# Gate and up of two feed-forwards by seven block products instead of eight

## The reference, cut to what matters

```
h = rms_norm(x, norm_g)                               # 1024 x 1024
ff = silu(h @ w_gate) * (h @ w_up)                    # 1024 x 2816
x = x + scale * (ff @ w_down)                         # scale 1.0 (ffn0) or 0.5 (ffn2)
```

## Time and profile before

| | |
|---|---|
| median of 3 runs | 3575.89 us |
| profiled execution | 3575.58 us |
| its span, first to last instruction | 3573.8 us |
| TensorE matmul busy | 3481.6 us, 97% |
| vector engine busy | 1467.3 us, 41% |
| GpSimd busy | 1134.1 us, 32% |
| scalar engine busy | 963.1 us, 27% |
| granted TensorE clock, mean | 0.989 |
| moved by DMA | 218.31 MB |

### The profile page before, as it was taken

One profiled execution on the slowest core, in us unless ns is written; L12 is line 12 of the kernel. 1 busy time (PEld: TensorE's weight loads), 2 busy tenths in 40 slices (PEclk: granted clock), 3 DMA queues, 4 the chain that ended last, 5 costly groups with the idle time before them and its releaser, 6 DMA issues.

```text
span 3573.8 us, 52859 instructions
## 1 busy us (share of the span) xinstructions
PE 3481.6 (97%) x20076; PEld 2931.2 (82%) x20076; DVE 1467.3 (41%) x2552; ACT 963.1 (27%) x1684; POOL 1134.1 (32%) x1499
## 2 busy tenths in 40 slices
PE   7999889999999999999999999999999999999998
PEld 5788778888888889899999878897777888888886
DVE  7966545211121263322122472837876521111214
ACT  5354433211111142111111333215663321111112
POOL 3433045322222353222222442310015532222323
PEclk9999899999999999999999999999999999999999
DMA  3112022111111121111111222111024211111113
GB/s 122 43 43 79 14 94 84 53 53 44 51 46 54 43 83 52 48 47 41 53 42 51 92 101 78 41 33 38 31 91 148 95 64 49 52 43 53 47 45 102
DMA packets 82740, 218.31 MB, mean 61 GB/s; under 512 B 20112, under 2 KB 20240, under 8 KB 82064
## 3 DMA queue, kind: packets, MB, share of 16 engines
q1 hardware_dynamic: 61936, 173.09, 15.4%
q10 hardware_dynamic: 20640, 42.95, 3.4%
HBM read 195.48 MB, written 19.46 MB: 60 GB/s over the span
## 4 chain that ended last, share of the span: by engine, by line
issue 60%; POOL 24%; PE 9%; DVE 4%; ACT 1%; POOLq 1%; DMA 0%; DVEq 0%; ACTq 0%; SPq 0%
POOL w_lo L582 24%; PE acc L744 2%; PE acc L745 2%; PE acc L746 2%; DVE cv_acc L1762 2%; PE acc L1294 0%; PE acc L1289 0%; POOLq L586 0%; PE acc L1411 0%; DVE ssq L693 0%; PE acc L1353 0%; PE acc L1420 0%; DVE cvo L1853 0%; PE acc L1428 0%; DVE tmp L705 0%
## 5 line engine op out<-in xcount | busy, mean ns | idle before, releaser
L582 POOL TENSOR_TENSOR w_lo<-w_raw,w_hi 128x256 fp32r<-128x256 f32 (+3 forms) x1480 | 1113.3, 783 | 2317.1 <-ACT w_hi L552 2316.9
L744 PE MATMUL acc<-h_hi,w_hi 128*128 128x512 f32 (+1 forms) x3520 | 1291.8, 367 | 16.5 <-issue 5.1
L745 PE MATMUL acc<-h_lo,w_hi 128*128 128x512 f32 (+1 forms) x3520 | 1283.9, 365 | 0.0
L746 PE MATMUL acc<-h_hi,w_lo 128*128 128x512 f32 (+1 forms) x3520 | 1283.2, 365 | 0.0
L744 PEld LDWEIGHTS acc<-h_hi,w_hi 128*128 128x128 f32 x3520 | 662.7, 188 | 127.6 <-issue 14.1
L745 PEld LDWEIGHTS acc<-h_lo,w_hi 128*128 128x128 f32 x3520 | 662.7, 188 | 106.0 <-issue 1.9
L746 PEld LDWEIGHTS acc<-h_hi,w_lo 128*128 128x128 f32 x3520 | 662.4, 188 | 106.1
L552 ACT CAST w_hi<-w_raw 128x1024 fp32r<-128x1024 f32 (+3 forms) x370 | 345.9, 935 | 1185.5 <-PE acc L746 1172.1
L1025 DVE TENSOR_TENSOR ff_hi<-tmp,acc 128x512 f32 (+3 forms) x154 | 94.5, 614 | 1070.5 <-PE acc L746 1039.1
L744 PE MATMUL acc<-ff_hi,w_hi 128*128 128x512 f32 (+1 forms) x1232 | 447.2, 363 | 6.4 <-POOL w_lo L582 3.2
L745 PE MATMUL acc<-ff_lo,w_hi 128*128 128x512 f32 (+1 forms) x1232 | 443.3, 360 | 0.0
(11 more groups left out here) (376 smaller groups left out, 3015.0 us busy)
## 6 DMA issues: line engine op xcount, KB each, us to landing
w_raw<-in_ffn_w_dram SPq DMA_DIRECT2D x94, 512.0 KB, 3.3
w_raw<-in_w_in_dram SPq DMA_DIRECT2D x60, 512.0 KB, 3.3
w_raw<-in_w_out_dram SPq DMA_DIRECT2D x32, 512.0 KB, 3.3
w_raw<-in_ffn_w_dram SPq DMA_DIRECT2D x48, 320.0 KB, 2.9
w_raw<-in_w_gate_dram SPq DMA_DIRECT2D x24, 512.0 KB, 3.3
w_raw<-in_w_up_dram SPq DMA_DIRECT2D x24, 512.0 KB, 3.3
w_raw<-in_ffn_w_dram SPq DMA_DIRECT2D x32, 384.0 KB, 3.0
gates_kept<-gstage ACTq DMA_DIRECT2D x32, 256.0 KB, 2.0
```

The source lines that it names most:

```text
L582: pool.tensor_tensor(w_lo[:, j, a:a + step], w_raw[:, j, a:a + step], w_hi[:, j, a:a + step].bitcast(F32), ALU.subtract).then_inc(split_do ...
L744: pe.matmul(bank, wh, rh, start=(k == 0), stop=False)
L745: pe.matmul(bank, wh, rl, start=False, stop=False)
L746: ins = pe.matmul(bank, wl, rh, start=False, stop=(k == seg.kt - 1))
```

## The change

Only ffn0 and ffn2 get the new scheme (`SEVEN`). In all three feed-forwards `FQ` becomes 4, 5, 5, 4, 4.

The first four tiles (`PLAIN`: three early ones and one in `up0`) are computed as before. The other 18 are taken two at a time: nine quads (`QUADS`). In a quad, gate (g = 0) or up (g = 1) is a product of a 2x2 block matrix of weights (two feature tiles x two halves of the inputs) with a 2x2 block matrix of activations (two halves of the inputs x two token chunks). It is computed by Strassen's scheme with seven products m1 to m7 of half depth (4 blocks of 128, 12 matmuls) instead of eight. For this

- the activations need five sums of blocks, s1, s3, s4, s6, s7, each of 4 tiles of 512 columns, high and low part. Each tile takes: DVE adds the high parts, POOL the low parts, DVE adds both to one whole, ACT takes the high part of it, DVE the low part. s1 and s3 lie where x lay, s4 beyond, s6 and s7 overwrite parts of h. `pe_mixed` therefore orders the last plain tile so that these parts are read first;
- five of seven weights per quad and matrix are sums or differences of two blocks (`weight_sum`, DVE, two slots `w_sum`). Highs (ACT) and lows (POOL) of 512 columns go through a ring of four, four products ahead (`AHEAD`);
- the products add up in three PSUM banks for each of gate and up (`BANKS`); m3 and m6 add onto m5's bank, m4 and m7 onto m2's, and must wait until the value so far was read (`reads`, `silu`);
- x goes to HBM (`x_kept`) during early_b and comes back behind the fourth last product; the gated units of all parts but the last (part 4) go to HBM (`ff_kept`) quad by quad and come back part by part, into `ff` and `h` in turn. The down products run after all gate and up work, part 4 first, then 0, 1, 2 and 3 (`DOWN_ORDER`).

The meta norm of ffn0 moves beside the down products. In ffn1 `up0` has now 2 pairs instead of 4, and eight squares follow each. New semaphores reuse old ones by an offset (`LATER`).

```diff
-FQ = [6, 6, 5, 5]
+FQ = [4, 5, 5, 4, 4]
+SUM_OF = {"m1": ((0, 0), 1, (1, 1)), "m5": ((0, 0), 1, (0, 1)), "m2": ((1, 0), 1, (1, 1)), "m3": ((0, 0), 0, None),
+          "m4": ((1, 1), 0, None), "m6": ((1, 0), -1, (0, 0)), "m7": ((0, 1), -1, (1, 1))}
...
+        def pool_seven(pool, name, seg, split):
...
+            if name.endswith("_early_b"):
+                pool.wait_ge(sem("lo_done"), KD * (u + 2))
+                for k in range(4):
+                    low_sum("s4", k)
+                split(0, 0)
+                split(0, 1)
+                for k in range(4):
+                    low_sum("s1", k)
+                split(1, 0)
+                split(1, 1)
+                return
+            for k in range(4):
+                low_sum("s3", k)
+            split(0, 0)
+            split(0, 1)
+            for k in range(4):
+                low_sum("s6", k)
+            for n in range(N_PRODUCTS):
+                low(n)
...
+        def pe_seven(pe, name, then, beside):
...
+            for n, (q, g, m) in enumerate(PRODUCTS):
+                pe.wait_ge(later("lows"), later_count("lows", name, n + 1))
...
+                if m == "m3":
+                    pe.wait_ge(reads, later_count("reads", name, 10 * q + 4 * g + 1))
+                if m == "m4":
+                    pe.wait_ge(reads, later_count("reads", name, 10 * q + 4 * g + 2))
...
+                for k in range(KD // 2):
...
+                    pe.matmul(bank, wh, rh, start=(k == 0 and m in ("m1", "m5", "m2")), stop=False, skip_group_check=True)
+                    pe.matmul(bank, wh, rl, start=False, stop=False, skip_group_check=True)
+                    ins = pe.matmul(bank, wl, rh, start=False, stop=(k == KD // 2 - 1), skip_group_check=True)
...
+        def act_seven(act, name, beside):
...
+            for e, (seg, i, c, f) in enumerate(early):
...
+                plain(seg, i, c, e % 3)
+                if not seg.again and (seg.name[-1] == "b" or i == EARLY[name] - 1) and c == len(seg.chunks) - 1:
+                    w_pair(act, seg, i)
+                if e in (2, 3, 4):
+                    for k in range(KD // 2):
+                        high_sum(BLOCK_SUMS[e - 2], k)
...
+                if m == "m1":
+                    act.wait_ge(later("products"), later_count("products", name, 1 + n + 1))
+                    act.wait_ge(sem("ff_" + name), 2 + 4 * q)
+                    act.copy(u_tile[:, 0, :] if g else G11, family(g, m)).then_inc(later("silu"), 1)
...
+        def dve_seven(dve, own, name, scale, beside):
...
+            def block_sums(which, ks):
...
+                elif which != "s4":
+                    dve.wait_ge(later("x_spilled"), later_count("x_spilled", name, 32))
+                for k in ks:
+                    high_part(which, k)
+                own.wait()
+                for k in ks:
+                    whole(which, k)
+                for k in ks:
+                    low_part(which, k)
...
+            for e, (seg, i, c, f) in enumerate(early_of(name)):
+                plain(seg, i, c, f, e % 3)
+                if e in (2, 3, 4):
+                    block_sums(BLOCK_SUMS[e - 2], range(KD // 2))
...
+            for n, (q, g, m) in enumerate(PRODUCTS):
+                if n + AHEAD < N_PRODUCTS:
+                    weight_sum(n + AHEAD)
+                if n == 0:
+                    block_sums("s7", range(2))
...
-            return list(enumerate(FIN_SQ))[6 * i:6 * i + 6]
+            return list(enumerate(FIN_SQ))[8 * i:8 * i + 8]
```

More of the change, by code:

```diff
@@ L48 @@
 LOW_PIECES = 4
+SEVEN = ("ffn0", "ffn2")
+QUADS = (FT - EARLY["ffn0"] - 1) // 2
+PLAIN = FT - 2 * QUADS
+DOWN_ORDER = (4, 0, 1, 2, 3)
+SUM_OF = {"m1": ((0, 0), 1, (1, 1)), "m5": ((0, 0), 1, (0, 1)), "m2": ((1, 0), 1, (1, 1)), "m3": ((0, 0), 0, None),
+          "m4": ((1, 1), 0, None), "m6": ((1, 0), -1, (0, 0)), "m7": ((0, 1), -1, (1, 1))}
+TURNS_OF_SEVEN = ("m1", "m5", "m2", "m3", "m4", "m6", "m7")
+LAST_SEVEN = ("m1", "m5", "m2", "m3", "m4", "m7", "m6")
+BLOCK_SUMS = ("s4", "s1", "s3", "s6", "s7")
+N_PRODUCTS = 14 * QUADS
+AHEAD = 4
+assert FQ[-1] == 4 and QUADS >= 2 and EARLY["ffn0"] == EARLY["ffn2"]
 CONST = {}
@@ L181, in halves, with seven @@
         add(name + "b", pairs, kt, chunks[-1:], src, lambda i, j, c: 3 * j + len(chunks) - 1, fine=True)
+    def seven(name, wg, wu, wd):
+        nonlocal raws
+        early([f"{name}_early_{x}" for x in "arb"], EARLY[name], CH1, pair(wg, wu))
+        add(f"{name}_up0", 1, KD, CH1, pair(wg, wu, EARLY[name]))
+        raws += QUADS
+        for part in DOWN_ORDER[:-1]:
+            add(f"{name}_down{part}", KD // 2, FQ[part], CH1, run(wd[part], 0))
+        part = DOWN_ORDER[-1]
+        halves(f"{name}_down{part}", KD // 2, FQ[part], CH1, run(wd[part], 0))
     def ffn(name, wg, wu, wd, chunks):
@@ new lines, in build_program, with later, later_count, ff_slot @@
+        UP_WEIGHTS = {"ffn0": (t["w_gate"], t["w_up"]), "ffn2": (t["ffn2_w1_2"], t["ffn2_w3_2"])}
+        def later(name):
+            return sem(LATER[name][0])
+        def later_count(name, ffn, n):
+            _, before, per = LATER[name]
+            return before + per * SEVEN.index(ffn) + n
+        def ff_slot(f):
+            return (f + 2) % 4
+        H_FIRST, H_SECOND = slice(META, META + 512), slice(META + 512, L)
+        def operand(m, k, whole=False):
+            if m in ("m1", "m3", "m4"):
+                hi, lo = ({"m1": s1_f, "m3": s3_f, "m4": s4_f} if whole else {"m1": s1, "m3": s3, "m4": s4})[m]
+                return hi[:, k, :], lo[:, k, :]
+            row, cols = {"m2": (k, H_FIRST), "m5": (k + KD // 2, H_SECOND), "m6": (k, H_SECOND), "m7": (k + KD // 2, H_FIRST)}[m]
+            hi, lo = h_f if whole else (h_hi, h_lo)
+            return hi[:, row, cols], lo[:, row, cols]
@@ new lines, in sevens, with ring @@
+        def sevens(q, g):
+            return LAST_SEVEN if (q, g) == (QUADS - 1, 1) else TURNS_OF_SEVEN
+        PRODUCTS = [(q, g, m) for q in range(QUADS) for g in range(2) for m in sevens(q, g)]
+        SUM_NO = {}
+        for n_, (_, _, m_) in enumerate(PRODUCTS):
+            if SUM_OF[m_][1]:
+                SUM_NO[n_] = len(SUM_NO)
+        SUMMED = list(SUM_NO)
+        def ring(n):
+            r = (n + 2) % AHEAD
+            return r // 2, slice(512 * (r % 2), 512 * (r % 2) + 512)
@@ L962, in pe_ffn, with pe_mixed @@
                         pe_slab(pe, down, i, j, (ff_hi, ff_lo))
+        def pe_mixed(pe, seg, freed):
+            blocks = (((0, range(KD // 2, KD)), (1, range(KD // 2))), ((0, range(KD // 2)), (1, range(KD // 2, KD))))
+            for turn, j in ((0, 0), (0, 1), (1, 1), (1, 0)):
+                if turn == 0:
+                    pe.wait_ge(split_done, LOW_PIECES * (seg.n0 + j + 1))
+                for c, ks in blocks[turn]:
+                    c0, w = seg.chunks[c]
+                    if turn == 0:
+                        pe.wait_ge(acc_free[j], seg.need[0, j, c])
+                    bank = acc[:, seg.bank(0, j, c), 0:w]
+                    for k in ks:
+                        wh, wl = w_hi[:, j, k * P:(k + 1) * P], w_lo[:, j, k * P:(k + 1) * P]
+                        rh, rl = h_hi[:, k, c0:c0 + w], h_lo[:, k, c0:c0 + w]
+                        pe.matmul(bank, wh, rh, start=(turn == 0 and k == ks[0]), stop=False, skip_group_check=True)
+                        pe.matmul(bank, wh, rl, start=False, stop=False, skip_group_check=True)
+                        ins = pe.matmul(bank, wl, rh, start=False, stop=(turn == 1 and k == ks[-1]), skip_group_check=True)
+                    if turn == 1:
+                        ins.then_inc(acc_full[j], 1)
+                if turn == 0 and j == 1:
+                    ins.then_inc(freed, 1)
@@ L2694, in _ @@
             act_turn(act, "ffn2", (SEG["out2a"], SEG["out2b"]))
[L2695 removed]
+            act_seven(act, "ffn2", nothing)
             act_turn(act, "fin2", last_of("ffn2"))
@@ L2717, in _ @@
             pe_mix1(pe)
-            pe_ffn(pe, "ffn0", CH1, "ffn1", lambda: pe_meta(pe))
+            pe_seven(pe, "ffn0", "ffn1", lambda: pe_meta(pe))
             pe_ffn(pe, "ffn1", CH2, "mix2", lambda: pe_fin(pe))
             pe_mix2(pe)
-            pe_ffn(pe, "ffn2", CH1, "fin2", nothing)
+            pe_seven(pe, "ffn2", "fin2", nothing)
             pe_mean(pe, "fin2", 1)
```

355 lines of the change are left out of this document (344 added, 11 removed).

## The result

The changed kernel takes 3586.16 us (median of 7 runs, 3585.95 to 3587.85), the kernel before 3574.72 us beside it (7 runs, 3570.33 to 3577.07): ratio 1.0035, 95% interval 1.0023 to 1.0046. The prediction was 3543 us, range 3514 to 3580: 43 us off, with the wrong sign. The profiled execution took 3587.48 us, 11.9 more than the 3575.58 of the one before.

What follows compares the result with a forecast made beforehand. TensorE's matmul count and new holes were taken to bound the changed stretches. From 3575.58 us: - 98.3 + 36 + 6 + 3 + 10 + 11 = -32.3, so 3543 us, range 3514 to 3580.

Steps and rivals of the forecast that it cites:

- Matmuls: Gate and up of both changed feed-forwards: 432 fewer matmuls at 0.2275 us, 98.3 us saved.
- Start: Start of each changed feed-forward: two queue-order holes and late reads, 18 us each, 36 for both; bounds 12 and 26 each.
- echo: After a TensorE hole, thirteen matmuls at the slow 1.2 GHz level, 2.6 us a hole; the first hole's hidden.
- rival A: Quads: GpSimd's instructions hold up the vector engine, making it the bound; 59 us in place of 6, 3596 us; chance 0.12.
- Quads: Ends of quads: late vector reads stall TensorE 0.4 us at each of 16 borders, 6 us in all.
- Last quad to down: After the last quad: seven vector operations make the down chunks late, 1.5 us each, 3 in all.
- Turns: Half b of the turns: bound by the vector engine's chain, so fewer matmuls there hardly shorten it; 10 us lost.
- ffn1: ffn1's norm: squares still open when up0 ends and a shorter down pair before the next wait; 11 us lost.
- B: Start of changed feed-forwards: s1 and s3 cost nothing, only the reads 3 us each; 3513 us; chance 0.13.
- C: Start and elsewhere: transfers meet in shared queues and enlarge the holes; 3569 us; chance 0.08.
- D: Products of the new scheme: each starts with a gap of 0.1 us, 25 us in all; 3568 us; chance 0.07.

Runs made afterwards that it cites:

- x_narrow: The changed kernel with every 512-wide GpSimd instruction of the new scheme split into two of 256: 3576.77 us, ratio 1.0004.
- x_nosums: The changed kernel without its five block sums of activations, the products reading h in their place: 3513.99 us, ratio 0.9828.
- x_turn4: The kernel before with parts of 6, 6, 6, 4 tiles instead of 6, 6, 5, 5: 3585.54 us, ratio 1.0027.
- both orders: The changed kernel with s1's and s3's sums interleaved with weight splits, casts before copies, s7's sums behind m5's and m2's reads: 3562.06 us, ratio 0.9967.

## Why the prediction was wrong

Point by point, both changed feed-forwards together:

- **Matmuls, - 98.3**: right; 19644 of them.
- **Start, 36 predicted, 72 measured** (36.2 and 35.9 by TensorE's count, 72.2 by removing the sums). This is the step that failed. The mechanism, two holes from the queue order and then late reads, stood; its size did not. In ffn0 the holes put up0 8.26 + 6.51 = 14.8 us late, 16.6 with the 9 slow matmuls between them (10.8 to 13.7 predicted, that echo taken as hidden), and the 11 behind them add 2.2: 18.8 where I took 15. The other 16.9 of the 35.7 us are the waits and echoes at the first products, where I took 3: m3 waited 7.76 us for the m5 read instead of 1.9, m6 another 2.49, and each of these two waits has 8 slow matmuls behind it.
- What I had wrong there is the vector engine's work ahead of that read. The step has only "six operations of s7, a weight sum and the m5 read" behind the last plain products, so it takes s6 as done. At "0.62 start to start" it would be: an estimate from this trace's 668.28 is 668.28 + 12 x 0.62 = 675.7, before the last plain product ends at 679.13. It took 13.8 us, 1.15 each, and ended at 682.1. The read, put by the step three products and 1.9 us behind the last plain product (8.2 + 1.9 = 10.1), ended 17.9 behind it. So it was not the price of contention that failed, 1.1 to 1.2 in the earlier trace rows and 1.16 on the mean in the stretch before the read; it was that s6 was left out and the price not charged to the whole stretch. Single rows beside 512-wide GpSimd instructions were longer (up to 1.79), and that is worth 3 us a start (x_narrow).
- The rule that I set beside the earlier trace rows (the Trainium skill, page "SBUF — State Buffer", section "Who interferes with whom": exclusion for the whole instruction) bears on this: by it the operation waits as long as GpSimd's instruction lasts, and in the traces single rows grow with the width, from 1.25 to 1.72. I took it to the quads as rival A; at the start I charged it to GpSimd's sums in the bounds of 12 to 26 us, and not to the vector engine's stretch before the reads.
- **Quads, 6 predicted**: 2 x 3.6 = 7 measured. Rival A's cause is real there, since halves bring TensorE back to no idle time, but its price was 0.4 a quad, not 3.3. The wait is where the step put it, before m3 of each quad, for the vector engine's read of m5:

```profile
742.16 0.47 PE L1224 MATMUL acc<-s_hi,w_hi 128*128 128x512 f32 x1 [0.19 <-DVE tmp L1494]
```

- **Last quad to down, 3**: 2 x 3.1 = 6, and not from the sums (x_nosums).
- **Turns, 10**: 10.1 by x_turn4.
- **ffn1, 11**: 17.9 from mean to mean, of which 2.9 belong to the turn (x_turn4 has 758.6 for 755.7): 15. The waits are where they were put, 8.02 at the mean (7 predicted) and 6.09 behind the first down pair (7 to 8).
- Sum with the measured terms: - 98.3 + 72 + 7 + 6 + 10 + 15 = + 12 us, against 11.4 by the medians.

**The rivals.** B (start hidden) fell; its 3513 is, by chance of arithmetic, what the kernel takes without sums. C fell: one half of the spill did take 14.2 us, but the two halves overlap, issued at 599.79 and 600.46, and GpSimd's first sum of s1 starts right behind the pieces before it, with no wait. x_nosums keeps all this traffic and has no holes at the start:

```profile
617.32 4.17 POOL L786 TENSOR_TENSOR w_lo<-w_raw,w_hi 128x256 fp32r<-128x256 f32 x4 [2.42 <-ACT w_hi L715]
621.45 6.36 POOL L746 TENSOR_TENSOR s_lo_f<-h_lo 128x512 f32<-128x512 f32 x4
...
x_kept<-x SPq DMA_DIRECT2D x2, 2112.0 KB, 9.3
x_kept<-x SPq DMA_DIRECT2D x2, 2048.0 KB, 14.2
```

D fell: the 312 us of quads lost 3.6 us in all, where a gap of 0.1 before each of some 114 products would be 11, and in x_narrow TensorE has no gap there. No rival had the case that came, a start of twice its price. A, the slower case with a related cause, stood at 0.12; the error was to let contention act in one place only.

## What to carry to other kernels

Trading matmuls for sums pays only what the other engines' queues leave of it: here 49 us of matmuls a feed-forward stood against 36 us at a start whose sums nothing covered, and the same change became 0.9% faster once the sums were interleaved with the splits, the wide GpSimd instructions halved and ffn1's parts kept longer. Before you say how late a read is, list everything that its engine does from the moment its inputs are free, and charge each operation by a row that has its neighbour in it (here 1.16 us and not 0.62). Where an engine works without a pause up to a read that TensorE awaits, reordering only moves the wait; take operations or contention away.

## What the runs showed of the hardware that I had not expected

- A vector operation of 128x512 with two SBUF inputs took 0.69 us alone, up to 1.28 beside 256-wide GpSimd instructions, and up to 1.79 beside 512-wide ones. Splitting the latter costs GpSimd time (185.43 for 150.68 us busy in 280 us) and still gained 9.4 us, about half of it in the quads.
- A longer wait did not echo more. After 8.26 us TensorE's matmuls start 0.427 us apart nine times (the 1.2 GHz level), then 0.23. The last of them and the first at the old pace:

```profile
638.79 0.59 PE L953 MATMUL acc<-h_hi,w_lo 128*128 128x512 f32 x1
639.21 0.39 PE L951 MATMUL acc<-h_hi,w_hi 128*128 128x512 f32 x1
```

  Eleven follow the 6.51 us wait, eight the 7.76 and eight the 2.49, and thirteen followed 4.85 in the earlier trace rows. Behind the 1.26, 2.22 and 2.35 us waits of the kernel with both orders there are none. The 2.6 us a hole of the prediction is one case of several.
